# Top-16 searches of a PEER layer two at a time: one operation for a pair where each search had its own

## The reference, cut to what matters

```python
s = jnp.einsum('thik,hink->thin', q, sub_keys).astype(jnp.float32)
v_half, i_half = lax.top_k(s, TOPK)
cand = (v_half[:, :, 0, :, None] + v_half[:, :, 1, None, :]).reshape(t, PEER_HEADS, TOPK * TOPK)
cand_idx = (i_half[:, :, 0, :, None] * N_KEYS + i_half[:, :, 1, None, :]).reshape(t, PEER_HEADS, TOPK * TOPK)
top_v, top_pos = lax.top_k(cand, TOPK)
idx = jnp.take_along_axis(cand_idx, top_pos, axis=-1)
g = jax.nn.softmax(top_v, axis=-1)
u = expert_u[idx]
act = jax.nn.gelu(jnp.einsum('thkd,td->thk', u, xb).astype(jnp.float32))
v = expert_v[idx]
return jnp.einsum('thk,thkd->td', (g * act).astype(xb.dtype), v)
```

## Time and profile before

| | us |
|---|---|
| median of 3 runs (2726.8 to 2734.45) | 2727.28 |
| the profiled execution | 2725.89 |
| its span | 2723.7 |
| TensorE busy in the span | 2352.0 |
| VectorE busy in the span | 1809.4 |

### The profile page before, as it was taken

How to read it: one execution, slowest core, us unless ns; L and a number is a source line. 1 busy time by engine, 2 the same in 40 slices (tenths; PEclk the granted TensorE clock), 3 DMA queues, 4 the chain that set the end, 5 groups by cost and what they waited for, 6 DMA issues and landing times.

```text
span 2723.7 us, 26660 instructions
## 1 busy us (share of the span) xinstructions
PE 2352.0 (86%) x8858; PEld 1471.6 (54%) x8858; DVE 1809.4 (66%) x3342; ACT 609.6 (22%) x1484; POOL 1142.5 (42%) x944
## 2 busy tenths in 40 slices
PE   6898888899989999899989989856999999999700
PEld 1354545444545644476668878746666666544300
DVE  0335777754201489777778997899677666677788
ACT  0112443522111112421321112168011101000010
POOL 0002222221000146766542234633557776777675
PEclk9889999999999999999999999878999999999955
DMA  7611110112364679999874578966999999999998
GB/s 265 235 31 31 55 39 23 39 55 89 122 224 169 221 267 330 379 372 393 318 268 176 203 269 330 398 213 224 389 405 395 400 390 400 391 388 398 350 358 302
DMA packets 236964, 701.58 MB, mean 258 GB/s; under 512 B 20912, under 2 KB 45616, under 8 KB 235568
## 3 DMA queue, kind: packets, MB, share of 16 engines
q0 software_dynamic: 112896, 411.09, 40.2%
q1 hardware_dynamic: 123232, 286.40, 28.9%
q10 hardware_dynamic: 720, 2.62, 0.2%
HBM read 686.93 MB, written 13.11 MB: 257 GB/s over the span
## 4 chain that ended last, share of the span: by engine, by line
PE 34%; DVE 22%; DMA 19%; POOL 12%; issue 9%; ACT 3%; DVEq 0%; SPq 0%; ACTq 0%; POOLq 0%
PE bank L892 15%; DMA arena<-in_peer_v,arena 9%; POOL arena L1665 5%; POOL arena L1657 5%; DMA arena<-in_peer_u,arena 4%; PE bank L746 4%; DVE arena L2014 2%; DVE arena L2036 2%; PE bank L787 2%; PE bank L1040 2%; DVE arena L1826 2%; DMA arena<-in_w_ada 2%; PE bank L705 2%; DMA arena<-in_w_ssd_out 2%; DVE arena L1974 1%
## 5 line engine op out<-in xcount | busy, mean ns | idle before, releaser
L1657 POOL DMA_INDIRECT arena<-in_peer_u,arena x384 | 499.0, 1299 | 757.2 <-DVE arena L2014 407.6
L2036 DVE SCALAR_TENSOR_TENSOR arena<-arena 128x1024 f32<-128x1024 f32 x381 | 496.7, 1304 | 137.4 <-DMA arena<-in_peer_v,arena 131.1
L2014 DVE CUSTOM_DVE_ANT_0 arena<-arena 128x1024 f32<-128x1024 f32 x384 | 475.0, 1245 | 151.0 <-DMA arena<-in_peer_u,arena 150.4
L1665 POOL DMA_INDIRECT arena<-in_peer_v,arena x384 | 444.9, 1159 | 251.5 <-DVE arena L2036 148.8
L892 PE MATMUL bank<-arena 128*128 128x512 f32 (+1 forms) x1472 | 507.5, 506 | 17.0 <-DMA arena<-in_w_in 6.1
L1110 PE MATMUL bank<-arena 128*128 128x256 f32 x2048 | 458.3, 382 | 22.6 <-ACT arena L1530 21.8
L1141 PE MATMUL bank<-arena 128*128 128x512 f32 x1024 | 453.2, 595 | 2.5 <-DMA arena<-in_peer_v 2.5
L1110 PEld LDWEIGHTS bank<-arena 128*128 128x128 f32 x2048 | 392.0, 192 | 105.4 <-issue 53.8
L892 PEld LDWEIGHTS bank<-arena 128*128 128x128 f32 x1472 | 282.4, 193 | 237.9 <-issue 196.4
L1141 PEld LDWEIGHTS bank<-arena 128*128 128x128 f32 x1024 | 195.5, 191 | 221.9 <-issue 215.5
L746 PE MATMUL bank<-arena 128*128 128x512 f32 x384 | 184.3, 627 | 7.9 <-ACT arena L1205 6.5
(11 more groups left out here) (242 smaller groups left out, 2371.4 us busy)
## 6 DMA issues: line engine op xcount, KB each, us to landing
arena<-in_peer_ut SPq DMA_DIRECT2D x128, 512.0 KB, 6.8
arena<-in_peer_v SPq DMA_DIRECT2D x128, 512.0 KB, 6.9
arena<-in_w_in SPq DMA_DIRECT2D x22, 2048.0 KB, 8.8
arena<-in_w_ada SPq DMA_DIRECT2D x12, 2048.0 KB, 8.0
arena<-in_w_ssd_out SPq DMA_DIRECT2D x8, 2048.0 KB, 16.9
arena<-in_w_query SPq DMA_DIRECT2D x8, 2048.0 KB, 8.6
arena<-in_w_fourier SPq DMA_DIRECT2D x4, 2048.0 KB, 7.7
arena<-in_w_out SPq DMA_DIRECT2D x4, 2048.0 KB, 14.0
```

The source lines that it names most:

```text
L1657: nc.gpsimd.indirect_dma_start(rowbuf[slot], None, a["peer_u"], bass.IndirectOffsetOnAxis(ap=entries(IDX, k), axis=0)).then_inc(row_in[slo ...
L1665: nc.gpsimd.indirect_dma_start(rowbuf[slot], None, a["peer_v"], bass.IndirectOffsetOnAxis(ap=entries(IDX, k), axis=0)).then_inc(row_in[slo ...
L2014: V.tensor_tensor_reduce(out=rowbuf[slot], in0=rowbuf[slot], in1=h2c if item < PH else h2a[:, item // PH - 1, :], scale=1.0, scalar=0.0, o ...
L2036: STT(pv, rowbuf[slot], w, pv, ALU.mult, ALU.add).then_inc(s("vc_used"), 1)
```

## The change

`top` takes one or two items. The selections (`best16`) stay one by one, as they were; the cast, the grid of sums, the subtraction, the masks, the comparison, the product and the sum (and, for gathered tiles, the expert number) are each one operation for both, with twice the elements. The subtraction becomes a tensor_tensor with the maximum broadcast, where it was a tensor_scalar. The scratch is laid out anew; `ij_w` and `d_w` trade places in the arena.

Whole tiles 3 and 4 of one head form a pair (8 pairs). Context heads 2 to 7 form three pairs, after steps 2, 14 and 26. Heads of tiles 1 and 2 form eight pairs: (0, 1) behind head 2 of the whole tiles, (2, 3) behind head 6, and (4, 5) to (14, 15) at steps 50, 82, 114, 146, 178 and 210. Each pair is searched where its first head was, so the second heads move forward: head 1 from behind head 4 to behind head 2, head 3 from step 34 to behind head 6, the others by 16 steps (6 in the context). A pair releases its waiters by 2 at its end.

```diff
-TOPS_AT = {2: 2, 8: 3, 14: 4, 20: 5, 26: 6, 32: 7}
+TOPS_AT = {2: (2, 3), 14: (4, 5), 26: (6, 7)}
...
-APART_TOP_BESIDE = {2: 0, 4: 1, 6: 2}
-APART_TOP_AT = {16 * n - 14: n for n in range(3, 2 * PH)}
+APART_TOP_BESIDE = {2: (0, 1), 6: (2, 3)}
+APART_TOP_AT = {16 * n - 14: (n, n + 1) for n in range(4, 2 * PH, 2)}
...
-        ij_w = [at(kb, 2 * PICKS).rearrange("p (t n) -> p t n", t=2) for kb in (109, 139.25)]
-        apart = (139.25 - 109) * KB
-        ij_pair = at(109, 2 * int(apart)).rearrange("p (h n) -> p h n", h=2)[:, :, 0:2 * PICKS].rearrange("p h (t n) -> p h t n", t=2)
-        d_w = at(140.25, 2 * PICKS).rearrange("p (t n) -> p t n", t=2)
+        ij_w = [at(kb, 2 * PICKS).rearrange("p (t n) -> p t n", t=2) for kb in (139.25, 140.25)]
+        ij_all = at(139.25, 4 * PICKS).rearrange("p (g n) -> p g n", g=4)
+        d_w = at(109, 2 * PICKS).rearrange("p (t n) -> p t n", t=2)
...
-        sw, sw2 = (at(118 + i, 256).rearrange("p (h n) -> p h n", h=2) for i in range(2))
-        cand, cand2 = at(120, 256), at(121, 256)
-        eq = at(122, 256).bitcast(BF16).rearrange("p (k n) -> p k n", n=TOPK)
+        sw2 = at(118, 256).rearrange("p (h n) -> p h n", h=2)
+        cands, cand2 = at(119, 512), at(121, 256)
         small = at(124, 12 * 32).rearrange("p (i n) -> p i n", i=12)
-        v16, pick = small[:, 0], small[:, 1]
-        i16, i16f = small[:, 2].bitcast(U32), small[:, 3, 0:TOPK].bitcast(BF16)
-        tv, tp = small[:, 4, 0:TOPK], small[:, 4, TOPK:].bitcast(U32)
-        tij = small[:, 5].bitcast(U32).rearrange("p (h k) -> p h k", h=2)
+        four = at(122, 4 * 64).rearrange("p (i n) -> p i n", i=4)
+        v16s, i16s, tijs, picks = four[:, 0], four[:, 1].bitcast(U32), four[:, 2].bitcast(U32), four[:, 3]
+        small64 = at(124, 64)
+        tvs, tps = small64[:, 0:32], small64[:, 32:64].bitcast(U32)
+        i16fs = small[:, 2].bitcast(BF16)
...
-            def top(item):
+            def scores_of(item):
 
                 t, h = divmod(item, PH)
                 if t in APART:
@@ -1982,29 +1982,43 @@
                     dve.wait_ge(s("fs_out"), 2 * h + 1)
                 src = (score_c[:, h * 256:h * 256 + 256] if t == 0 else score_a[item - PH] if t in APART
                        else score_w[:, t - 3, h * 256:h * 256 + 256])
-                src = src.rearrange("p (h n) -> p h n", h=2)
-                for half in range(2):
-                    best16(v16[:, 16 * half:16 * half + 16], i16[:, 16 * half:16 * half + 16],
-                           src[:, half, :], sw2[:, half, :])
-                CP(i16f, i16)
-                ch(TT(cand.rearrange("p (a b) -> p a b", a=TOPK),
-                      v16[:, 0:16].unsqueeze(2).broadcast_to([P, 16, 16]),
-                      v16[:, 16:32].unsqueeze(1).broadcast_to([P, 16, 16]), ALU.add))
-                best16(tv, tp, cand, cand2)
-                over = entries(DTAB, item * TOPK, TOPK) if t not in WHOLE else d_w[:, t - 3, TOPK * h:TOPK * h + TOPK]
-                TS(over, tv, tv[:, 0:1], None, ALU.subtract)
-                ch(TT(tij, tp.unsqueeze(1).broadcast_to([P, 2, TOPK]), masks[:], ALU.bitwise_and))
-                e4 = eq.rearrange("p (h k) n -> p h k n", h=2)
-                ch(TT(e4, places[:].unsqueeze(2).broadcast_to([P, 2, TOPK, TOPK]),
-                      tij.unsqueeze(3).broadcast_to([P, 2, TOPK, TOPK]), ALU.is_equal))
-                ch(TT(e4, e4, i16f.rearrange("p (h n) -> p h n", h=2).unsqueeze(2).broadcast_to([P, 2, 16, 16]),
-                      ALU.mult))
+                return src.rearrange("p (h n) -> p h n", h=2)
+
+            def top(*items):
+
+                n = len(items)
+                views = [x[:, 0:2 * n * TOPK].rearrange("p (h q k) -> p h q k", h=2, q=n) for x in (v16s, i16s, tijs, picks)]
+                v16, i16, tij, pick = views
+                flat = lambda x: x[:, 0:2 * n * TOPK].rearrange("p (g k) -> p g k", g=2 * n)
+                tv, tp = (x[:, 0:n * TOPK].rearrange("p (q k) -> p q k", q=n) for x in (tvs, tps))
+                cand = cands[:, 0:256 * n].rearrange("p (q a b) -> p q a b", q=n, a=TOPK)
+                for q, item in enumerate(items):
+                    src = scores_of(item)
+                    for half in range(2):
+                        best16(v16[:, half, q, :], i16[:, half, q, :], src[:, half, :], sw2[:, half, :])
+                CP(i16fs[:, 0:2 * n * TOPK], i16s[:, 0:2 * n * TOPK])
+                ch(TT(cand, v16[:, 0].unsqueeze(3).broadcast_to([P, n, TOPK, TOPK]),
+                      v16[:, 1].unsqueeze(2).broadcast_to([P, n, TOPK, TOPK]), ALU.add))
+                for q in range(n):
+                    best16(tv[:, q, :], tp[:, q, :], cands[:, 256 * q:256 * q + 256], cand2)
+                t, h = divmod(items[0], PH)
+                over = (d_w[:, :, TOPK * h:TOPK * h + TOPK] if t in WHOLE else
+                        entries(DTAB, items[0] * TOPK, n * TOPK).rearrange("p (q k) -> p q k", q=n))
+                TT(over, tv, tv[:, :, 0:1].broadcast_to([P, n, TOPK]), ALU.subtract)
+                ch(TT(tij, tp.unsqueeze(1).broadcast_to([P, 2, n, TOPK]), masks[:].unsqueeze(2).broadcast_to([P, 2, n, TOPK]),
+                      ALU.bitwise_and))
+                e4 = cands[:, 0:256 * n].bitcast(BF16).rearrange("p (g k m) -> p g k m", g=2 * n, m=TOPK)
+                place = places[:, 0:4:3 - n, :]
+                ch(TT(e4, place.unsqueeze(2).broadcast_to([P, 2 * n, TOPK, TOPK]),
+                      flat(tijs).unsqueeze(3).broadcast_to([P, 2 * n, TOPK, TOPK]), ALU.is_equal))
+                ch(TT(e4, e4, flat(i16fs).unsqueeze(2).broadcast_to([P, 2 * n, TOPK, TOPK]), ALU.mult))
                 if t in WHOLE:
-                    V.tensor_reduce(ij_pair[:, :, t - 3, TOPK * h:TOPK * h + TOPK], e4, AX.X, ALU.add).then_inc(s("topw_done"), 1)
+                    V.tensor_reduce(ij_all[:, :, TOPK * h:TOPK * h + TOPK], e4, AX.X, ALU.add).then_inc(s("topw_done"), n)
                 else:
-                    ch(V.tensor_reduce(pick, eq, AX.X, ALU.add))
-                    STT(entries(IDX, item * TOPK, TOPK), pick[:, 0:16], float(NKEY), pick[:, 16:32],
-                        ALU.mult, ALU.add).then_inc(s("topk_done"), 1)
+                    ch(V.tensor_reduce(flat(picks), e4, AX.X, ALU.add))
+                    half = picks[:, 0:n * TOPK], picks[:, n * TOPK:2 * n * TOPK]
+                    STT(entries(IDX, items[0] * TOPK, n * TOPK), half[0], float(NKEY), half[1],
+                        ALU.mult, ALU.add).then_inc(s("topk_done"), n)
 
...
-                    top(TOPS_AT[j])
+                    top(*TOPS_AT[j])
...
-                        if APART_TOP_AT[j] == NORM_TOPS - PH:
+                        if APART_TOP_AT[j][0] == NORM_TOPS - PH:
                             dve.wait_ge(s("pv_done"), 2)
-                        top(PH + APART_TOP_AT[j])
+                        top(*(PH + n for n in APART_TOP_AT[j]))
...
             context_steps(8)
             for h in range(PH):
-                top(3 * PH + h)
-                top(4 * PH + h)
+                top(3 * PH + h, 4 * PH + h)
                 context_steps(CTX_BESIDE[h])
                 if h in APART_TOP_BESIDE:
-                    top(PH + APART_TOP_BESIDE[h])
+                    top(*(PH + n for n in APART_TOP_BESIDE[h]))
...
```

More of the change, by code:

```diff
@@ L255 @@
 NORM_STEP = max(PICKS + APART_LEAD, START_LAST)
-NORM_TOPS = PH + min(n for j, n in APART_TOP_AT.items() if j > NORM_STEP)
+NORM_TOPS = PH + min(pair[0] for j, pair in APART_TOP_AT.items() if j > NORM_STEP)
 RESULT_1_AT = NORM_STEP + 8
@@ L334, in layer_kernel @@
         stat = sb("stat", [P, 64])
-        places = sb("places", [P, 2, TOPK], U32)
+        places = sb("places", [P, 4, TOPK], U32)
         masks = sb("masks", [P, 2, TOPK], U32)
@@ L1742, in _ @@
             CP(selb[:], sel[:])
-            CP(places[:, 1, :], shp[:, 6, 0:TOPK])
-            TS(places[:, 0, :], shp[:, 6, 0:TOPK], float(TOPK), None, ALU.mult)
+            row16 = shp[:, 6, 0:TOPK].unsqueeze(1).broadcast_to([P, 2, TOPK])
+            CP(places[:, 2:4, :], row16)
+            TS(places[:, 0:2, :], row16, float(TOPK), None, ALU.mult)
             V.memset(masks[:, 0, :], TOPK * (TOPK - 1))
```

## The result

The changed kernel takes 2705.9 us (median of 5 runs, 2701.96 to 2719.83) against 2727.28: ratio 0.9934, 95% interval 0.9912 to 0.9956, or 18 us less. (The ratio goes by all five executions of each, whose means are 2709.9 and 2728.0 us; the medians lie 21 us apart. The profiled execution, at 2719.83 us, is the slowest of its five; the one of before took 2725.89. So only 6 of the 18 us lie between these two traces, and no stage length of them may be read to a microsecond: the stage of the blocks took 674.7 us in this profile and 665.7 in e1_again's, of the same kernel.

The account below looks back on a forecast made before the run. VectorE bounds searches and build, TensorE the block stage, then gathers alone; DMA engines set the end. -12.1 + 2.6 + 0.6 + 12.1 - 7.4 = -4.2 us gave 2721.7, forecast 2723.1 against the median; range 2709 to 2737.

Parts of the forecast that it names:

- the first rival: Block stage: the block stream fills the gathers' gap, so long pauses lose no DMA time; 2711 us, chance 0.22.
- the early half: Merged pairs up to the expert product: -12.1 saved, +2.6 given back, +0.6 in the token mixer, together -9 us.
- the late half: Merged pairs from step 82 on: +12.1 for pauses, -7.4 for the hole behind TensorE's end, together +4.7 us.
- Before the build, -9.5: Search stage: eleven merged pairs save 12.1 us of VectorE, 2.6 given back to row waits and fuller DMA engines.
- The token mixer, +0.6: Before step 31, six searches instead of five delay ScalarE's dot products by 4.3 us, against 3.71 to spare.
- +12.1: Block stage, steps 82 to 226: five pairs' 16.1 us pauses starve the gathers, 8.4 for four and 3.7 after the build.
- -7.4: TensorE's end: the last search leaves step 226, where the block stream ran out, removing 7.4 us of lost DMA time.
- pauses that cost nothing: Block stage, merged pairs only there, arena off the block: pauses are free, leaving -5 to -7 us.
- Both marks that I set for being wrong: Wrong if the build's start moves by less than 6 us, or build-to-end span grows by more than 12 or shrinks.

Follow-up runs that it names:

- e1_again: The changed kernel unaltered, on another chip, for a second profile and more times: 2715.01 us, ratio 0.9931 to the kernel before.
- e5: The kernel before plus 128 unused bytes per partition ahead of the arena, which then starts at byte 24320 (95 x 256): 2700.07 us, ratio 0.9912.
- e7: The kernel before with its arena moved to 32 bytes past a 256-byte block (24352): ratio 1.0000.
- e4: The kernel before with head 15's search moved from step 226 to right behind head 14's at step 210: ratio 0.9976.
- e10: The changed kernel with single searches at their old steps up to the expert product, merged pairs from step 82, arena off the block (24448): ratio 0.9990.
- e6: The changed kernel plus 128 unused bytes per partition ahead of the arena, putting it off the block (24448): 2726.17 us, ratio 0.9992.
- e9: The changed kernel with merged pairs only up to the expert product, single searches from step 82, arena off the block (24448): ratio 0.9986.
- e11: The kernel before with the arena on a block (24320) and head 15's search moved from step 226 to 210, none merged: ratio 0.9912.
- e2_placed: The changed kernel's order of searches with the kernel before's operations, two single searches back to back, off the block: ratio 1.0066.
- e3: The changed kernel with merged pairs only up to the expert product and single searches from step 82 on, arena on a block: ratio 0.9894.

## Why the forecast was short by 14 us: its steps against the runs

**What was missing.** This is the step that failed: the sum had no term for the DMA rate, and took the 410 GB/s of a full stretch as given. The place of the arena is worth 16 to 25 us, all of the gain within its interval; with the place as before, the pairs give -2.1 us (-5.5 to +1.4). So the forecast's -4.2 fits the pairs, and not the kernel: 2705.9 lies outside the range of 2709 to 2737, and near the first rival's 2711 for a reason that isn't its own. The rival wanted a DMA share near 1 behind pairs; it is 0.86 to 0.92 in the rows above. That -4.2 came near -2.1 is in part luck: apart, the early half gave -3.8 for -9 and the late half -2.7 for +4.7, two misses that cancel. With the arena on a block in both, the changed kernel (0.9934, 0.9931) is if anything 5 or 6 us slower than before (0.9912): the intervals overlap, so that isn't shown.

The rate, not the share, was the thing to read: at a share of 1.01 in both, the stage moved 395 GB/s before and 402 in e5. (In the earlier trace rows I also passed over slices 15 to 18, 1022 to 1294 us, which are 9s too; no term rested on them.) The Trainium skill, DMA: Bandwidth & Descriptors, section "How a descriptor splits into AXI transactions", says that a descriptor is cut at 256-byte boundaries and that one which starts off a boundary pays for the unused bytes of its first cut, counted in units of 32 bytes. It says so of reads; here it is the written side that moved, and to carry the rule over is my own step. An estimate by it: a row 128 bytes off costs 132 units for 128, 3.1% more. The traces are near that, with medians of 161 to 164 ns for 159 (1.3 to 3.1%) and means of 165.5 to 165.8 for 160.2 to 160.6 (3.2% or so). For 32 bytes off the estimate is 129 units, 0.8% more; e7's rows took 164 ns and its time did not move, so here the measurement decides.

**Before the build, -9.5.** Right in its stage. From the first whole tile's search to the build's first comparison, kernels off the block take 364.3, 365.1, 363.4 and 363.3 us with single searches (before, e4, e7, e10) and 355.6 and 354.3 with pairs (e6, e9): -9.1. On a block it is 362.7 and 363.6 (e5, e11) against 352.3 to 359.3 (five kernels with pairs, mean 356.0): -7.1.

**The token mixer, +0.6.** This term was mis-sized: as TensorE's waiting it is +7. TensorE's wait for ScalarE's clearing of the banks, in us, times and longest, from 900 to 1425 us, before and after:

```profile
PE bank L725 <- ACT arena L1343: 12.3, 6, 3.4
```

```profile
PE bank L724 <- ACT arena L1342: 19.1, 6, 10.5
```

The seven kernels with merged context pairs show 18.0 to 19.3 us with a longest of 9.8 to 11.2; before, e4, e5, e7, e10 and e11, without, show 11.0 to 12.9 and 3.4. e2_placed, with searches at the pairs' places but not merged, shows 19.8 and 11.6: it is the place that costs, not the merging. Ahead of it, ScalarE's wait for the dot products, which ended at 1047.90 in the earlier trace rows:

```profile
1057.82 0.22 ACT L1331 ACTIVATE arena<-arena 128x16 f32<-128x16 f32 x1 [27.99 <-DVE arena L2028]
```

It ends 9.9 us later, not 4.3. VectorE's work from 916 us (917 after) to that instant grew by 5.2 us (114.5 to 119.7), as counted; but I let 0.7 of it vanish into waits, and its idle time grew instead, from 17.4 to 21.1 us. Of the 9.9 us ScalarE's spare 3.7 covers its part, and the rest stands in TensorE's way. The first whole tile's search begins later with merged context pairs than without in kernels of one chip, by 8 us (1426.0 and 1425.5 against 1415.0 and 1420.0), by 9 (1434.0 and 1434.1 against 1422.5 and 1427.5) and by 3 (e1 and e3, 1421.6 and 1428.3, against e4's 1422.0); but kernels whose searches stand alike up to there also lie up to 7 us apart in these figures (e1 and e3). -9.1 and +7 make -2, against e9's measured -3.8 (-7.9 to +0.5). That the context pairs alone cost this in time was not tried.

**The block stage and TensorE's end, +12.1 and -7.4.** Right as DMA time. I take (1.03 - share) x length from each search's start to 15 us past its end. Before: 7.9 us over nine searches and 8.1 behind the last, 16.0. Off the block with pairs: 19.1 (e6) and 20.1 (e10), 3.9 a pair. Pauses +11.7, end -8.1, together +3.6 against the +4.7 forecast. In time e10 has -2.7 (-6.8 to +1.4), below it: this excludes the forecast's +4.7 and doesn't exclude pauses that cost nothing (-5 to -7), so off the block the price of the pauses in time is open. All the terms as measured make -9.1 + 7 + 3.6 = +1.5, just above e6's interval; some of them weigh less in time than in their view. e4's -6.6 is the end's term with one double pause (forecast -5, measured as DMA time about -4). The last search, before and then e5, both to 15 us past its end:

```profile
2561.80:2585.50 23.70, 9.90 (x24) 4.05 (x22) 23.04 (x54) 0.00 (x0) 12.91 (x11) 0.77 0.69 246
```

```profile
2531.40:2555.10 23.70, 23.70 (x57) 10.52 (x56) 21.34 (x51) 0.00 (x0) 12.35 (x9) 1.00 1.01 395
```

This also tells why the pairs look dearer once the arena is on a block. There VectorE gets its rows sooner, the step of the last search comes 30 us earlier, TensorE is still at work, and the hole that the pairs were to remove is gone already. By the same measure e5 loses 7.1 us in all and the changed kernel 21.7 (e1: 20.7): +14, where it was +3.6. In time, e1 less e3_early, the same two kernels' difference on one chip, is +7 us by the medians and +10 by the ratios, in the same direction, though the intervals overlap; and moving the last search gives nothing there (e11). A run of the late pairs alone on a block was not made.

**The marks.** The lengths of the merged operations, the 16.1 us of a gathered pair (16.2) and the pauses of 15 us came as written. The 15 us right behind the pairs had shares of 0.86, 0.81, 0.81, 0.86 and 0.87 in the first profile, where I wrote 0.85 or less, and 0.85, 0.84, 0.80, 1.00 and 0.84 in e1's: one of ten is the first rival's picture. TensorE's end, which was to come earlier by the build's lead, came at 2576.4 us, 5 later, and in e1's profile at 2563.1, 8 earlier. Both marks that I set for being wrong were met: the build's start moved by 3.1 us, not 6 (4.3 in e6), by the token mixer's term; and the span from the build to the end shrank by 2.7, by the DMA rate (in e6 it grew by 5.4, inside the bounds). By my own marks, then, the prediction did not hold for this kernel.

## What to carry to other kernels

A diff that changes the size of any allocation moves all that is allocated behind it: work out where the DMA buffers begin, before and after, ahead of any argument on instructions. Where DMA engines are full, read the plateau in GB/s beside the busy share, since a share of 1 looks the same at 410 and at 420 GB/s. And to price a change, hold its side effects fixed: one unused tensor of 128 bytes gave more (24 us) than the whole rewrite of the search with the arena off the block (2 us, and up to 5.5 within its interval).

## What the runs showed of the hardware

Rows of 4096 bytes written to buffers that start on a multiple of 256 bytes of the partition took a median of 159 ns in one DMA engine; with a start 128 or 32 bytes off the medians were 161 to 164 ns. Where the engines were full this made 409 to 410 GB/s of 418 to 420. On a kernel that keeps them busy (a share of 0.88 to 1.01) in its last 800 us, it was worth 16 to 25 us of 2730. Whether the place of the source matters as well wasn't tried.
